# Hybrid decoder step on one core: the key halves and value halves of the cache pages are loaded apart

## The reference

```python
past = (cache_a_kv[l][page_table].reshape(db, past_len, 2, H_A, HEAD),    # per position: [k1|k2] x 4 heads, then v x 4 heads
        cache_b_kv[l][page_table].reshape(db, past_len, 4, DH_B), ...)     # per position: k_cmp, v_cmp, k_sel, v_sel
...
s = jnp.einsum('bqhcd,bkhcd->bchqk', qb, kf) * scale                       # group A: two maps of each head
p = masked_softmax(s, k_pos[None, :] <= pos[:, None])
w = p[:, 0] - lam * p[:, 1]
return jnp.einsum('bhqk,bkhv->bqhv', w, vf)
...
ss = jnp.einsum('bqhd,bqnpd->bqhnp', qf, kg) * scale                       # group B: selected blocks of k_sel, v_sel
o_sel = jnp.einsum('bqhk,bqkd->bqhd', ps, vg)
```

## Time and profile before

| what | value |
|---|---|
| median of 3 runs | 1788.45 us (1780.99 to 1790.61) |
| profiled execution, its own time | 1780.37 us |
| profiled execution, span from first to last instruction | 1777.9 us |
| mean granted TensorE clock | 0.967 |
| decode stage, groups' transfers issued by SP | 1003.4 us to 1511.6 us |
| TensorE busy in the whole span | 1619.5 us (91%) |

### The profile page before, as it was taken

The page is one execution under the profiler, slowest core; times in us unless marked ns, Lnnn a source line. Parts: engine busy times, 40 slices in busy tenths (PEclk is TensorE's granted clock), DMA queues, the critical chain, the costliest instruction groups (busy, mean ns, idle before and its releaser), DMA issues. The chain is left out here.

```text
span 1777.9 us, 39056 instructions
## 1 busy us (share of the span) xinstructions
PE 1619.5 (91%) x14840; PEld 1256.8 (71%) x14840; DVE 788.5 (44%) x1554; ACT 612.5 (34%) x1410; POOL 139.5 (8%) x219
## 2 busy tenths in 40 slices
PE   6999999999899889998996798899898899789998
PEld 5888888777678757776665566666666667577776
DVE  4222221254137544344345445566565565763321
ACT  4312111242113313312214355555455555642210
POOL 3000000035100010000003000000000000110010
PEclk9999999999999999998998699999999999899999
DMA  7556555687633234337235679999889889663554
GB/s 212 173 174 203 180 190 148 189 298 231 203 113 118 72 109 132 113 107 206 89 96 210 224 292 377 336 351 370 297 316 355 306 301 373 251 222 106 169 178 151
DMA packets 219160, 379.58 MB, mean 214 GB/s; under 512 B 42301, under 2 KB 122206, under 8 KB 218174
## 3 DMA queue, kind: packets, MB, share of 16 engines
q1 hardware_dynamic: 210462, 350.38, 58.4%
q0 software_dynamic: 7520, 24.09, 4.0%
q10 hardware_dynamic: 992, 2.62, 0.4%
HBM read 344.47 MB, written 40.71 MB: 217 GB/s over the span
## 5 line engine op out<-in xcount | busy, mean ns | idle before, releaser
L372 PE MATMUL pj_ps<-pj_whi,pj_xhi 128*128 128x512 f32 (+1 forms) x1024 | 413.1, 403 | 9.5 <-PEq L95 6.0
L373 PE MATMUL pj_ps<-pj_wlo,pj_xhi 128*128 128x512 f32 (+1 forms) x1024 | 398.7, 389 | 0.0
L374 PE MATMUL pj_ps<-pj_whi,pj_xlo 128*128 128x512 f32 (+1 forms) x1024 | 397.6, 388 | 0.0
L297 DVE TENSOR_TENSOR pj_wlo<-pj_w,pj_whi 128x1024 fp32r<-128x1024 f32 (+1 forms) x128 | 155.8, 1217 | 441.6 <-ACT pj_whi L255 440.1
L255 ACT ACTIVATE pj_whi<-pj_w 128x1024 fp32r<-128x1024 f32 (+1 forms) x128 | 132.2, 1033 | 501.1 <-DMA pj_w<-in_w_in 500.8
L372 PEld LDWEIGHTS pj_ps<-pj_whi,pj_xhi 128*128 128x128 f32 x1024 | 195.3, 191 | 69.4 <-issue 31.7
L374 PEld LDWEIGHTS pj_ps<-pj_whi,pj_xlo 128*128 128x128 f32 x1024 | 195.4, 191 | 39.8
L373 PEld LDWEIGHTS pj_ps<-pj_wlo,pj_xhi 128*128 128x128 f32 x1024 | 195.6, 191 | 33.5
L1905 ACT ACTIVATE fr_kT<-da_tp 128x512 f32<-128x512 f32 x200 | 119.3, 597 | 165.2 <-PE da_tp L1779 162.3
L2015 DVE COPY fr_kT<-da_tp 128x512 f32<-128x512 f32 x128 | 88.4, 691 | 80.3 <-PE da_tp L1779 80.1
L1779 PE MATMUL da_tp<-all_ident,fr_front 128*128 128x128 f32 x640 | 96.8, 290 | 21.8 <-DMA fr_front<-in_cache_a_kv 12.2
(11 more groups left out here) (563 smaller groups left out, 2168.0 us busy)
## 6 DMA issues: line engine op xcount, KB each, us to landing
fr_front<-in_cache_a_kv SPq DMA_DIRECT2D x128, 512.0 KB, 6.3
da_pa<-in_cache_a_kv SPq DMA_DIRECT2D x128, 512.0 KB, 6.4
pj_w<-in_w_in SPq DMA_DIRECT2D x119, 512.0 KB, 4.6
px_pages<-in_cache_b_kv SPq DMA_DIRECT2D x256, 128.0 KB, 2.5
fr_front<-in_cache_b_kv SPq DMA_DIRECT2D x128, 128.0 KB, 6.5
da_pb<-in_cache_b_kv SPq DMA_DIRECT2D x128, 128.0 KB, 6.5
proj<-pj_out SPq DMA_DIRECT2D x52, 256.0 KB, 4.9
fr_kT<-in_w_out SPq DMA_DIRECT2D x16, 512.0 KB, 4.4
```

The lines of the kernel that those rows point to most:

```text
L297: dve.tensor_tensor(self.wlo[:, r, :, 0:n], self.w[:, r, :, 0:n], self.whi[:, r, :, 0:n], ALU.subtract).then_inc(self.wlo_ready, 1)
L372: pe.matmul(acc, hi, high, start=kc == 0, stop=False)
L373: pe.matmul(acc, hi, low, start=False, stop=False)
L374: last = pe.matmul(acc, lo, high, start=False, stop=kc == KC - 1)
```

## The change

`load_group` is split into two functions. `load_keys` asks for columns 0 to 511 of the four pages of group A (rows of 2 KB), and its wait is for `turned`, which TensorE raises at the end of each `turn`: it is met when the four heads' keys of group m-4 have been turned. `load_values` asks for the pages of group B and for columns 512 to 1023 of group A, and its wait is the old one, `summed`. Each reads the page numbers for itself. From group 6 on SP issues the keys of group m and then the rest of group m-2 (`BEHIND` = 2); the rests of the last two groups follow at the end. TensorE waits for `values_loaded` in `values`, in addition to what it waited for. No byte more or less is loaded, and nothing that is computed changes.

```diff
--- before.py
+++ after.py
@@ -1037,19 +1037,34 @@
         yield
 
 
-def load_group(nc, d, k, sp, m, a, b, wait=None):
-
-    _, pages = nc.values_load_multi_w_load_instructions(
+def page_ids(nc, d, k, m):
+
+    return nc.values_load_multi_w_load_instructions(
         k.page_rows[0:1, 4 * m:4 * m + 4], engines=[mybir.EngineType.SP],
-        min_val=0, max_val=d.cache_b.shape[0] - 1)
+        min_val=0, max_val=d.cache_b.shape[0] - 1)[1]
+
+
+def load_keys(nc, d, k, sp, m, a, wait=None):
+
+    pages = page_ids(nc, d, k, m)
     if wait is not None:
         sp.wait_ge(*wait)
     for i in range(4):
-        sp.dma_start(a[:, i, :], d.cache_a[bass.ds(pages[i], 1), :, :]
-                     .rearrange("a p n -> p (a n)")).then_inc(k.a_loaded[m % RING], 16)
+        sp.dma_start(a[:, i, 0:512], d.cache_a[bass.ds(pages[i], 1), :, 0:512]
+                     .rearrange("a p n -> p (a n)")).then_inc(k.keys_loaded[m % RING], 16)
+
+
+def load_values(nc, d, k, sp, m, a, b, wait=None):
+
+    pages = page_ids(nc, d, k, m)
+    if wait is not None:
+        sp.wait_ge(*wait)
     for i in range(4):
         sp.dma_start(b[:, i, :], d.cache_b[bass.ds(pages[i], 1), :, 256:512]
                      .rearrange("a p n -> p (a n)")).then_inc(k.b_loaded[m % RING], 16)
+    for i in range(4):
+        sp.dma_start(a[:, i, 512:1024], d.cache_a[bass.ds(pages[i], 1), :, 512:1024]
+                     .rearrange("a p n -> p (a n)")).then_inc(k.values_loaded[m % RING], 16)
 
 
 def decode_masks(pool, k, zeroed, made):
@@ -1182,7 +1197,8 @@
                 sp.dma_start(k.page_rows[:], d.page_table.rearrange("(a b) n -> a (b n)", a=1)).then_inc(table_loaded, 16)
                 sp.wait_ge(table_loaded, 16)
                 for m in range(EARLY):
-                    load_group(nc, d, k, sp, m, k.early_a[m], k.early_b[m])
+                    load_keys(nc, d, k, sp, m, k.early_a[m])
+                    load_values(nc, d, k, sp, m, k.early_a[m], k.early_b[m])
                 for c in range(NSEC):
                     t, sec = c // 3, c % 3
                     sp.wait_ge(finished, c + 1)
@@ -1639,6 +1655,8 @@
     dve_turns = [sum(1 for m, j in turns if m < n and j % 2 == 1) for n in range(N + 1)]
     a_steps = [n for n in range(N) if steps[n][1] != "win"]
     a_of = {n: a for a, n in enumerate(a_steps)}
+    page_step = [n for n in range(N) if steps[n][1] == "page"]
+    BEHIND = 2
 
     tp_order = []
     for n in range(N + 2):
@@ -1679,7 +1697,7 @@
         gs, gt, go = s.ps("gs", [P, 512]), s.ps("gt", [P, 4, P]), s.ps("go", [P, 4, HEAD])
         guest = LateTiles(nc, d, k, s, (gs, gt, go))
 
-        a_loaded, b_loaded = k.a_loaded, k.b_loaded
+        keys_loaded, values_loaded, b_loaded = k.keys_loaded, k.values_loaded, k.b_loaded
         win_loaded = s.sem("win_loaded")
         spread = s.sem("spread")
         dve_step = s.sem("dve_step")
@@ -1713,19 +1731,28 @@
         with nc.Block() as block:
             @block.sync
             def _(sp):
+                def load_rest(m):
+                    load_values(nc, d, k, sp, m, pa[m % RING], pb[m % RING], (summed, page_step[m - RING] + 1))
+
                 for n, (b, what, p) in enumerate(steps):
                     if what == "page":
                         m = b * NG + p
                         if m < EARLY:
                             continue
-                        old = next((x + 1 for x in range(N) if steps[x][1] == "page"
-                                    and steps[x][0] * NG + steps[x][2] == m - RING), None)
-                        load_group(nc, d, k, sp, m, pa[m % RING], pb[m % RING], (summed, old) if old else None)
+                        if m < RING:
+                            load_keys(nc, d, k, sp, m, pa[m])
+                            load_values(nc, d, k, sp, m, pa[m], pb[m])
+                            continue
+                        load_keys(nc, d, k, sp, m, pa[m % RING], (turned, first_turn[page_step[m - RING]] + HA))
+                        if m - BEHIND >= RING:
+                            load_rest(m - BEHIND)
                     elif what == "win":
                         if b:
                             sp.wait_ge(summed, n - G + 1)
                         sp.dma_start(pw[:], d.b_win[b, :, :].rearrange("(i p) n -> p i n", p=P)).then_inc(win_loaded, 16)
 
+                for m in range(DB * NG - BEHIND, DB * NG):
+                    load_rest(m)
                 sp.wait_ge(summed, at[DB - 1, "win", 0] + 1)
                 out.load_w(sp, 2)
                 sp.wait_ge(guest.stored, 16 * PT)
@@ -1767,7 +1794,7 @@
                     j = jobs[n][x]
                     if what == "page" and j in (0, HA):
                         m = b * NG + p
-                        pe.wait_ge((b_loaded if j else a_loaded)[m % RING], 64 * (m // RING + 1))
+                        pe.wait_ge((b_loaded if j else keys_loaded)[m % RING], 64 * (m // RING + 1))
                     if x == 0 and what == "win":
                         pe.wait_ge(win_loaded, 16 * (b + 1))
                     bank_free(("key", n, x))
@@ -1836,7 +1863,9 @@
                     pe.wait_ge(pb_copied, n + 1)
                     pe.wait_ge(o_copied, n)
                     if what == "page":
-                        r = (b * NG + p) % RING
+                        m = b * NG + p
+                        r = m % RING
+                        pe.wait_ge(values_loaded[r], 64 * (m // RING + 1))
                         for c in range(4):
                             for h in range(HA):
                                 pe.matmul(po[32 * h:32 * h + 8, 0:HEAD], pT[:, n % 2, c, h, :],
@@ -3742,7 +3771,8 @@
             k.hot = a.sb("hot", [8, 2, P])
             k.late = a.sb("late", [8, DB * NS + 8])
             k.late_w = a.sb("late_w", [P, P])
-            k.a_loaded = a.sems("a_loaded", RING)
+            k.keys_loaded = a.sems("keys_loaded", RING)
+            k.values_loaded = a.sems("values_loaded", RING)
             k.b_loaded = a.sems("b_loaded", RING)
             with Stage(nc, "ap") as p:
                 k.q_early = p.sb("q_early", [P, HA + HB, P * EARLY_T])
```

## The result

The changed kernel takes 1868.07 us (median of 4 executions, 1865.04 to 1875.84), the kernel before 1789.53 us on the same chip (4 executions): a ratio of 1.044, interval 1.040 to 1.048, so slower. The profiled execution took 1865.04 us where the one of before took 1780.37, which is 84.7 us more; the prediction said 83.6 us more, 1864 us.

The account below looks back on a forecast made before the run. TensorE was taken as the bound, SP and DMA close behind; after the change, SP. The profiled 1780.4 us plus 81.7 for the stage and 2 for the output projection's first tile gave 1864 us; range 1825 to 1900.

Parts of the forecast that it names:

- SP becomes the bound: Decode stage: SP's 9.1 to 10.2 us a group can't hide under the 8.20 us pace; chance 0.80.
- 9.7 us a group: SP's occupied time per group in the decode stage, taken as the middle between 9.1 and 10.2 us.
- The floor: SP's time for a group without waits, three fours and two readings: 9.22 us, or 9.1 with shortest fours.
- The excess over the floor: SP's mean occupied time above its no-wait time per group: 0.70 us before, from long single issues and the windows' transfers.
- the upper end of 10.15: SP's time per group if the twelve issues are lengthened in proportion: 9.1 + 0.70 x 12/8 = 10.15 us.
- The waits of the earlier trace go: TensorE's 12.2 us of waits for keys vanish through earlier asking; with the clock, a possible gain of 12 to 16 us.
- New waits at group B's keys, 90 to 105 us: TensorE would wait at the turning of group B's keys for transfers from `in_cache_b_kv`, some 90 to 105 us.
- rival (2): Decode stage: SP and the lower clock both bind, adding 20 to 60 us, so 1885 to 1925 us; chance 0.08.
- Rival (3): Decode stage: SP's issues overlap or shrink, fitting under TensorE's pace of 7.9 us a group; 1766 us, chance 0.05.
- rival (4): No change that shows, within 0.5%: SP at 8.2 to 8.4 us a group gives back the gain; chance 0.03.
- The end of the stage: Last value product of the decode stage ends at 1614.1 us, 81.7 later; output projection's first tile costs 2 us more.
- 2-KB rows don't bind: DMA in the decode stage: 270 GB/s asked for, 369 possible with 2-KB rows; binding only at 7.1 us a group.

Follow-up runs that it names:

- the two readings more: The kernel before, with each group's page numbers read three times instead of once, extra readings unused: 1845.98 us, ratio 1.036.
- after, unchecked: The changed kernel, still with two readings a group, without the bounds checks of its readings: 1778.93 us, 0.992 of the kernel before.

## Why the prediction was right, point by point

- **SP becomes the bound**: shown. It never waits in the stage; adding time on SP alone makes such a loss (the two readings more), and taking register instructions away alone removes it (after, unchecked). In the four kernels in which SP's occupied time is above 8.2 us the time follows it: 62 times the excess over 8.2 is 10, 46, 95 and 102 us, and the profiled executions took 7, 50, 85 and 100 us more than that of the kernel before.
- **9.7 us a group**: 9.73 measured. The two parts were each off. The floor is 9.02 and not 9.1 to 9.22, because the added reading stands in place of a gap and I had counted both (0.20 too much; the lower figure is a slip as well, since with the shortest fours that sum is 9.17). A reading is 1.33 to 1.35 us, not 1.55; the rest is the gap that stands between fours anyhow. The excess over the floor was 0.70 before and is 9.73 - 9.02 = 0.71 after: it did not grow with the number of transfers, as the upper end of 10.15 took it to, nor shrink. That the middle value hit within 0.03 us is luck: the floor in it was 0.1 to 0.2 too high, and the excess over the floor, 0.5 to 0.6, as much too low.
- **The waits of the earlier trace rows go**: shown, by the list. But the prediction put this down to asking two steps earlier, and that is at best the smaller part of it: in the kernels where SP fits, the split by itself takes most or all of these waits away, and the early asking adds 7.5 us in one kind and 2 us, not told apart from nothing, in the other. The size, 12 to 16 us, was a little low: it is 19 us against the kernel before, of which one reading fewer and no checks are a part, since they make SP fit; the missing checks alone give nothing (1792.39 us).
- **New waits at group B's keys, 90 to 105 us**: the place is right, the size was 73.9 us. The term left out was the clock: at 0.92 TensorE's work in the stage is 30 us longer and fills time that I had put down as waiting. So rival (2)'s mechanism is there, but SP never waits for TensorE, and it adds nothing to the sum.
- **Rival (3)**, faster when a group of SP is under 7.9 us: the mechanism holds, and the runs put the point between 7.76 and 8.36 us. At 7.76 and 7.37 us the changed kernel is faster, at 8.36 it is level (rival (4)'s place, at 1.004), at 9.73 slower. It is no sharp point: at 7.76 us 3.5 us of waits are left, at 7.37 us 0.2. It was no case of the change as made.
- **The end of the stage**: the last product was forecast to end at 1614.1 us and ended at 1614.65, by terms that cancel. The stage's first issue came 6.0 us earlier in this execution (997.41; other kernels show 1000 to 1009, so this is scatter). Against it stand 2.0 us more of issuing (603.4 us for 601.4), 1.1 us because the last turn came 1.5 us behind SP's last issue and not 0.4, and 3.4 us in the tail (12.3 us for 8.9), from ACT's wait for `h_c`, which I had looked for behind the last product and on GpSimd alone. Behind the last product it is 248.6 us to the span's end where it was 245.5: 3.2 us, against the 2 us I took. So from first issue to last product it is 617.2 us where it was 529.0: 88.2 us more, not 81.7. The total was right to 1 us, its parts to some 6 us.
- **2-KB rows don't bind**: shown by the kernel with such rows, at 1.003.

The fit that the prediction took from the Trainium skill ("DMA: Bandwidth & Descriptors", "Anatomy of one DMA") is stated there for transfers that GpSimd issues, while SP issues these. Nothing of the forecast was worked out from it.

The Trainium skill ("DMA: Bandwidth & Descriptors", "Issuing engines are not separate DMA queues") calls the sequencer's time for initiating a DMA usually small relative to the DMA itself. The trace agrees for one transfer, 0.33 us of issue beside 3.9 us to landing. It does not hold for a stage: twelve issues with the register instructions between them, and two readings, take 9.02 us at the least, more than the 8.2 us in which TensorE works off their data.

## What to carry to other kernels

Before a transfer is split, add up what its queue is occupied with in one iteration (the issues, and the reading of addresses into registers ahead of them) and set it against the pace of the engine that bounds the stage; the queue's waits show the slack, and here 1.9 us of it met 3.4 us of addition. Spare first what isn't a transfer: registers kept and checks dropped took 2.4 us of 9.7 and turned a loss of 4% into a gain of 1%. Where an engine waits for the first part of a large transfer, split it so that this part stands first in the queue, provided the queue has room for the added issues; that, more than the earlier request, took the waits away.

## What the hardware showed that I had not expected

The issue of a transfer on SP went by the number of rows and not by bytes: 0.333 us for 128 rows of 1, 2 or 4 KB, 0.543 us for 256 rows of 2 KB. That is not all that a transfer costs the queue: from one four to the next with only the ordinary gap between them are 1238.11 - 1236.00 = 2.11 us in the changed kernel, so 0.53 us each, with the register instructions ahead of each. Twelve times 0.53 and two readings of 1.35 make up the 9.02 us. On GpSimd an issue takes 0.547 us. Reading four page numbers costs 1.33 to 1.35 us with their bounds checks and 1.0 to 1.1 us less without; the table load in it is only 0.30 us. So the checks of four numbers cost SP as much as two transfers.
